# Seven calls that multiply ones by constants taken out of a two-block kernel

## The reference

```
def hybrid_layer(x, ...):                      # twice
    u = x * (1 + scale) + shift
    proj = u @ w_in                            # one wide projection, split in nine parts
    a = silu(layer_norm(conv31(a1 * sigmoid(a2))));  y_a = (a * silu(a_gate)) @ w_a_out
    y_b = (gb * conv3(gc * xb) * silu(b_gate)) @ w_b_out
    q = rms_norm(q_lat) @ w_uq                 # 8 heads of 64 + 32, rope on the 32
    kv = rms_norm(kv_lat) @ w_ukv
    y_c = (causal_attention(q, kv) * silu(c_gate)) @ w_c_out
    out = (g_a*y_a + g_b*y_b + g_c*y_c) @ w_o
    return layer_norm(ALPHA * x + gate * out)

def second_block(x, ctx, ...):
    h = rmsnorm(x) * (1 + sc) + sh             # norm "n0"; mLSTM over context and latents
    x = x + g * mlstm(h, hc)
    h = rmsnorm(x) * (1 + sc) + sh             # norm "n1"; Fourier branch
    x = x + g * fourier(h)
    return rmsnorm(x)                          # final norm "nf"
```

## Time and profile before

| | us |
|---|---|
| median of 3 timed runs | 2338.91 |
| lowest and highest | 2335.74, 2339.73 |
| the profiled execution, its time | 2344.25 |
| its span, first to last instruction | 2342.5 |
| PE busy | 2239.9 (96%) |
| DVE busy | 1454.8 (62%) |
| POOL busy | 1077.5 (46%) |
| ACT busy | 847.1 (36%) |
| mean granted clock of PE | 0.983 of full |

### The profile page before, as it was taken

How to read it: one execution, slowest core, us unless ns; L and a number is a source line. 1 busy time by engine, 2 the same in 40 slices (tenths; PEclk the granted TensorE clock), 3 DMA queues, 4 the chain that set the end, 5 groups by cost and what they waited for, 6 DMA issues and landing times.

```text
span 2342.5 us, 30567 instructions
## 1 busy us (share of the span) xinstructions
PE 2239.9 (96%) x11066; PEld 1834.5 (78%) x11066; DVE 1454.8 (62%) x2357; ACT 847.1 (36%) x1387; POOL 1077.5 (46%) x1273
## 2 busy tenths in 40 slices
PE   6899999999999999999999999998999999999998
PEld 3688777888778877788867888887877878788886
DVE  5889966564478986665358777555675766522322
ACT  2443335222353333422245444344343444432221
POOL 1555435565446543666534445441344344443343
PEclk8999999999999999999999999999999999999999
DMA  8342214664243222454322233233234242222222
GB/s 309 122 121 81 70 62 139 224 202 158 72 144 108 81 64 63 141 165 151 111 80 79 86 104 108 71 124 116 81 124 137 89 127 76 73 73 72 72 76 77
DMA packets 93205, 259.83 MB, mean 111 GB/s; under 512 B 10128, under 2 KB 11536, under 8 KB 92944
## 3 DMA queue, kind: packets, MB, share of 16 engines
q1 hardware_dynamic: 71392, 210.23, 28.8%
q10 hardware_dynamic: 21680, 47.79, 5.7%
HBM read 237.01 MB, written 20.97 MB: 110 GB/s over the span
## 4 chain that ended last, share of the span: by engine, by line
PE 52%; issue 21%; POOL 13%; DVE 10%; ACT 2%; DMA 1%; POOLq 0%; ACTq 0%; DVEq 0%; SPq 0%
PE bank L2135 16%; PE bank L2136 16%; PE bank L2137 15%; POOL t L422 13%; DVE t L1791 3%; DVE t L1577 1%; DVE t L1226 1%; PE bank L2188 1%; DMA t<-w_ada 1%; PE bank L2553 1%; PE bank L2373 1%; PE bank L2271 1%; DVE t L1230 0%; PE bank L2382 0%; PE bank L2211 0%
## 5 line engine op out<-in xcount | busy, mean ns | idle before, releaser
L422 POOL TENSOR_TENSOR t<-t,t 128x256 fp32r<-128x256 f32 x1208 | 1025.1, 880 | 1177.4 <-ACT t L485 1176.9
L2135 PE MATMUL bank<-t,t 128*128 128x512 f32 (+1 forms) x3056 | 1175.3, 385 | 31.5 <-DVE t L1226 9.4
L2136 PE MATMUL bank<-t,t 128*128 128x512 f32 (+1 forms) x3056 | 1147.8, 376 | 0.0
L2137 PE MATMUL bank<-t,t 128*128 128x512 f32 (+1 forms) x3056 | 1146.2, 375 | 0.0
L2135 PEld LDWEIGHTS bank<-t,t 128*128 128x128 f32 x3056 | 580.6, 190 | 160.3 <-issue 16.6
L2137 PEld LDWEIGHTS bank<-t,t 128*128 128x128 f32 x3056 | 579.0, 189 | 106.0
L2136 PEld LDWEIGHTS bank<-t,t 128*128 128x128 f32 x3056 | 580.8, 190 | 102.6 <-issue 3.5
L485 ACT ACTIVATE t<-t 128x1024 fp32r<-128x1024 f32 x302 | 317.2, 1054 | 279.6 <-PE bank L2137 232.9
L1290 DVE SCALAR_TENSOR_TENSOR t<-t,t,t 128x512 f32<-128x512 f32 x168 | 154.1, 937 | 103.2 <-DMA t<-w_ada 63.0
L1577 DVE SCALAR_TENSOR_TENSOR t<-t,t,t 128x512 f32<-128x512 f32 x240 | 206.1, 859 | 6.7
L1230 DVE SCALAR_TENSOR_TENSOR t<-t,bank 128x512 f32<-128x512 f32 x112 | 76.7, 685 | 157.0 <-ACT t L1183 59.9
(11 more groups left out here) (252 smaller groups left out, 1689.0 us busy)
## 6 DMA issues: line engine op xcount, KB each, us to landing
t<-blocks SPq DMA_DIRECT2D x306, 512.0 KB, 3.6
t<-w_ada SPq DMA_DIRECT2D x144, 256.0 KB, 2.7
t<-w_ada SPq DMA_DIRECT2D x20, 512.0 KB, 11.6
xm_park<-t ACTq DMA_DIRECT2D x16, 384.0 KB, 2.3
s_park<-t ACTq DMA_DIRECT2D x16, 384.0 KB, 2.4
t<-xm_park ACTq DMA_DIRECT2D x16, 384.0 KB, 4.4
t<-s_park ACTq DMA_DIRECT2D x16, 384.0 KB, 5.3
xc_park<-t ACTq DMA_DIRECT2D x16, 256.0 KB, 2.6
```

What stands on the lines that cost most here:

```text
L422: low = pool.tensor_tensor(w_lo[slot][:, part], w_raw[slot][:, part], w_hi[slot][:, part].bitcast(F32), ALU.subtract)
L2135: pe.matmul(out, wh, xh, start=start, stop=False)
L2136: pe.matmul(out, wh, xl, start=False, stop=False)
L2137: return pe.matmul(out, wl, xh, start=False, stop=stop)
```

## The change

All seven calls of `keep_busy` and the function itself are taken out. In the query heads the wait for "kv_std" stays. No other instruction changes on any engine; lines behind the function move up.

```
--- before.py
+++ after.py
@@ -2226,11 +2226,6 @@
                     mm = pe.matmul(bank[:, 128 * j:128 * (j + 1)], row, quarters[:, 0:128], start=True, stop=True)
                 mm.then_inc(pe_done, p(*label, "spread"))
 
-            def keep_busy(bank, n):
-
-                for _ in range(n):
-                    pe.matmul(banks[bank][:], ones[:], vec[:, 0:512], start=True, stop=True)
-
             def context_tile(c, middle=None):
 
                 b = AB["x", 0, c]
@@ -2289,9 +2284,7 @@
             first_scale(0)
             for l in range(L1):
                 if l:
-                    keep_busy(5, 1)
                     spread(banks[6], tmp[2], (l - 1, "x"))
-                    keep_busy(5, 2)
                 first = [banks[0], banks[1], banks[4]][:2 if l else 3]
                 first_chunks(first, B_QL(l), [(l, "q_lat", j) for j in range(3)],
                              lambda k: Dn(l, "uL", k), middle=(lambda: first_scale(1)) if l == 0 else None)
@@ -2326,7 +2319,6 @@
                 for h in range(1, HEADS):
                     if h == 6:
                         pe.wait_ge(act_done, A(l, "kv_std"))
-                        keep_busy(2, 4)
 
                     if h >= 4:
                         pe.wait_ge(act_done, A(l, "q", h - 4))
@@ -2600,9 +2592,7 @@
             context_tile(0, lambda: spread(banks[6], tmp[2], (L1 - 1, "x")))
             context_tile(1)
             norm_sums(range(KT), S, ("n0",), sq_t, 5)
-            keep_busy(7, 1)
             spread(banks[5], tmp[2], ("n0",))
-            keep_busy(7, 2)
             for k in range(KT):
                 pe.wait_ge(dve_done, Dn("n0", "uL", k))
                 for c in range(2):
```

## The result

| | median, us | runs |
|---|---|---|
| before | 2339.22 (2335.74 to 2341.28) | 7 |
| changed | 2347.16 (2344.62 to 2350.05) | 7 |
| ratio | 1.0036, 95% interval 1.0025 to 1.0048 | |

The changed kernel is 7.9 us slower, outside the 0.2% that a measurement can tell; the forecast was 2347.4.

The account below looks back on a forecast made before the run. PE, busy 96% of the span, and its clock were taken to bound the kernel. Five places summed to 9.6 us, less 1.1 for falls already paid: net +8.5, 2347.4 us, range 2340.5 to 2352.5.

Parts of the forecast that it names:

- The price of a gap: PE idle after removal: following work runs at half clock, losing 2.1 us per gap, 1.7 low end, 2.5 high.
- heads of layer 0: Query heads, PE idle 6.4 us ahead of head 6: clock falls, +2.1 us; layer 1, idle 4.6 us, also +2.1.
- the fall at 1284.39: Profile before: a 1.84 us gap ending at 1283.83, then 3.41 us at clock 0.50; one of four rows averaged.
- Layer-1 norm, +1.8: Layer 1's input norm: products behind the reciprocal's spread have no slack, +2.1 us, less 0.3 for an earlier spread.
- the second rival: Clock falls everywhere, but later waits for DVE's taps or POOL's weight splits swallow the loss: 0 to 4 us, chance 0.09.
- n0 and n1, 1.65 and 1.9: Second block's first and second norms: 1.4 us each after 0.7 slack, plus 0.25 and 0.5 for a slow spread.
- The slow spread, +0.9: Second block's norms: the reciprocal's spread may meet low clock, +0.9 us on the path, as at the final norm.
- The discount of 1.1 us: Layer 0's heads: about half the timed executions before probably already pay 2.1 us at the 2.96 us gap, so -1.1.
- the sum of 9.6: All five places on the profiled execution: 2.1 + 2.1 + 1.8 + 1.65 + 1.9 = 9.6 us, 2344.25 to 2353.8.
- The first rival: Only the two heads pay, since the spread keeps the clock at the norms: 2.8 us, 2341.7, chance 0.12.
- The third: Faster: removed passes ahead of each norm's spread had delayed waiting work, up to 2 us in all, 2336.9; chance 0.05.
- The fourth: All places: these fp32 matmuls never counted as work for the clock; no change, 2338.9, chance 0.04.

## Why the prediction was right

The time (2347.4 against 2347.16) and the main mechanism were right: the clock fell at all five places, behind the gaps that were named, and stood at 0.50 for 4.2 to 6.0 us of dense work. At four places the time was lost; at the fifth, the layer-1 norm, the cost was mis-sized. Point by point:

- That PE's idle time takes the place of the calls, released by the same DVE operation: 6.55 and 4.72 us measured, 6.4 and 4.6 forecast.
- The price of a gap, 2.1 us with a top of 2.5: heads of layer 0 +1.98, of layer 1 +2.77. The top was too low; a low stretch covered 6.0 us of work there, 3.0 us lost. One of the rows that it was taken from, the fall at 1284.39, was put at 1.7 us. That is work lost on PE and not time: the fall cost nothing, as said above.
- Layer-1 norm, +1.8: mis-sized. The products did lose 1.6 to 2 us, but PE's wait for ACT near 658 gave them back: +0.13 in the profile, and no cost with only these calls out. This is the second rival, the loss swallowed by a later wait, true at one place in five. The spread did start 0.32 us sooner behind the reciprocal, as forecast, but the saving was half of that: its last part had run at full clock before (1.92 us against 2.08), and DVE got its result 3.12 us after the reciprocal began (627.90 to 631.02), against 3.28 (629.23 to 632.51), 0.16 us. That the spread is at half clock with the calls in place as well was read from one execution; it is not so in five others.
- n0 and n1, 1.65 and 1.9: 2.96 and 2.38 in the profile. The slow spread, +0.9, came at both, where a quarter and half of it were reckoned with; and the low stretch behind n0 covered 5.45 us. In timed runs of the norms alone the mean cost was less, +3.1 for both.
- The discount of 1.1 us for a fall that the kernel before has in some executions: the fall is shown by the profile of the kernel with only the layer-1 norm changed. Five such falls in seven profiles at 1.25 to 1.49 us make a mean of 1.0, near the term.
- So the sum of 9.6 was met by a sum of 10.2 whose terms differ by up to 1.7 us from the forecast ones, and the profiled executions differed by 5.4 us, not 9.6. That the median came within 0.3 us of the forecast is luck; the sign and the size of some 8 us are not.
- The first rival (only the heads pay) fell by the run with the norms' calls out, +3.1 us (ratio above 1.0007). The third (faster) has its small place at the layer-1 norm, 0.16 us at the spread, and nothing more. The 1.5 us behind the wait near 658 were in no rival. The fourth (these matmuls don't count for the clock) fell by the whole result.

## What to carry to other kernels

Before taking out work that "nobody reads", look at what PE's clock does without it: waits of 1.5 to 6.5 us that PE had to sit out anyway cost another 2 to 3 us here at four of five places, since the work behind them ran at half clock. Filling paid elsewhere in this kernel too, most clearly where PE idled 4.06 us ahead of dense work; cheap filling (one column of weights) did as well as a full one. And what PE loses is only paid if nothing downstream was waiting on something else: read the wait that comes next, even 14 us later. A wait that is shortened in this way may also spare the fall of the clock behind it.

## What the runs showed that was not expected

- The clock can be kept with matmuls that make one output row: 512 moving columns by one weight column, at a pass of 0.59 us, left it at 1.00 from 1223 to 1240.
- The same gap in the same kernel keeps or loses the clock from one execution to the next (2.96 us in the heads: kept in the profile of before, lost in that of the kernel with only the layer-1 norm changed). One profile is therefore no measure of a kernel's clock losses: the two profiled executions differ by 5.4 us where the medians differ by 7.9.
- Each half of the filling at the norms (ahead of the spread or behind it) could go without a cost that the runs can tell (ratios 0.9998 and 1.0001, each to about 0.001), while both together cost 3.1 us.
- The low clock came with all filling in place, behind waits of at most 0.95 us (norm n1, kernel with only the layer-1 norm changed).
- A low stretch of 3.4 us can cost 1.5 us (659.75) or nothing (1284.39).
